# How an MoE stage numbers its slots and gathers its small experts: sixteen dealt pieces, rows at partitions 32 to 95

## The reference

```python
scores = sigmoid(x @ w_router)                     # 520 x 64
# of 8 groups of 8 experts the best 4 are kept, then the best 8 experts of a token
idx    = top_k(where(group_kept, scores + bias, -inf), 8)
gates  = w_sel / sum(w_sel) * 2.5
for each expert e, for each token t that chose it:
    y[t] += gate * (silu(x[t] @ w1[e]) * (x[t] @ w3[e])) @ w2[e]     # 1024 -> 256 -> 1024
```

## Time and profile before

| | us |
|---|---|
| median of three runs | 1242.86 |
| the profiled execution | 1241.34 |
| its span, from first to last instruction | 1239.5 |
| PE busy in the span | 1145.6 (92%) |
| PEld / DVE / ACT / POOL busy | 763.2 / 411.7 / 257.2 / 175.6 |

### The profile page before, as it was taken

One profiled execution on the slowest core, in us unless ns is written; L12 is line 12 of the kernel. 1 busy time (PEld: TensorE's weight loads), 2 busy tenths in 40 slices (PEclk: granted clock), 3 DMA queues, 4 the chain that ended last, 5 costly groups with the idle time before them and its releaser, 6 DMA issues.

```text
span 1239.5 us, 21052 instructions
## 1 busy us (share of the span) xinstructions
PE 1145.6 (92%) x8302; PEld 763.2 (62%) x8302; DVE 411.7 (33%) x1016; ACT 257.2 (21%) x564; POOL 175.6 (14%) x208
## 2 busy tenths in 40 slices
PE   7999997999987999889999899998999989989965
PEld 6888645877865688567656565555555556555411
DVE  0359997122067325711221111111211212111124
ACT  1101324022051315011222222221212212212200
POOL 3120040000000000202122122122221222211100
PEclk9999998999999999899999999999999999999977
DMA  9530304034048352619999999999999999999496
GB/s 330 226 136 1 153 12 170 1 135 153 1 141 322 132 216 91 241 51 337 358 378 375 369 376 379 368 376 358 370 370 359 373 378 358 376 359 363 182 357 268
DMA packets 66313, 319.16 MB, mean 257 GB/s; under 512 B 10473, under 2 KB 16833, under 8 KB 39629
## 3 DMA queue, kind: packets, MB, share of 16 engines
q1 hardware_dynamic: 51269, 278.60, 59.5%
q0 software_dynamic: 13568, 35.48, 8.4%
q10 hardware_dynamic: 1424, 4.35, 0.9%
HBM read 300.15 MB, written 29.36 MB: 266 GB/s over the span
## 4 chain that ended last, share of the span: by engine, by line
PE 68%; DMA 15%; DVE 14%; SPq 1%; issue 1%; ACT 1%; DVEq 0%; POOLq 0%
PE psum L744 62%; DMA arena<-in_w_e_dram 10%; DVE act_mem L1698 7%; PE psum L759 6%; DMA arena<-y_rows 3%; DVE mk_mem L1857 2%; DMA arena<-in_w_in_dram 1%; SPq L539 0%; DVE act_mem L1795 0%; DVE act_mem L1712 0%; DVE rstd L1786 0%; DVE act_mem L1793 0%; DVE act_mem L1763 0%; SPq L494 0%; SPq L493 0%
## 5 line engine op out<-in xcount | busy, mean ns | idle before, releaser
L744 PE MATMUL psum<-arena,act_mem 128*32 128x128 f32 (+6 forms) x4800 | 517.0, 365 | 20.8 <-DMA arena<-in_w_e_dram 16.5
L744 PEld LDWEIGHTS psum<-arena,act_mem 128*32 128x32 f32 (+5 forms) x4800 | 266.3, 125 | 210.7 <-issue 118.6
L744 PE MATMUL psum<-act_mem,arena 128*128 128x260 f32 (+1 forms) x1728 | 352.7, 366 | 9.2 <-DMA arena<-in_w_o_dram 3.8
L744 PEld LDWEIGHTS psum<-act_mem,arena 128*128 128x128 f32 x1728 | 306.2, 192 | 53.0 <-DMA arena<-in_w_o_dram 4.7
L759 PE MATMUL psum<-ident,act_mem 96*128 96x96 f32 (+8 forms) x484 | 77.7, 291 | 19.1 <-POOL ident L557 6.8
L667 POOL DMA_INDIRECT y_rows<-act_mem,idx_y x40 | 45.2, 1130 | 323.1 <-DVE idx_x L2074 173.0
L2086 DVE TENSOR_SCALAR act_mem<-psum,act_mem 96x512 f32<-96x512 f32 (+1 forms) x40 | 29.9, 748 | 156.0 <-PE psum L744 156.0
L1698 DVE SCALAR_TENSOR_TENSOR act_mem<-act_mem,wcb 128x511 f32<-128x511 f32 (+29 forms) x120 | 77.7, 725 | 0.0
L759 PEld LDWEIGHTS psum<-ident,act_mem 96*128 96x128 f32 (+8 forms) x484 | 57.5, 175 | 32.3 <-issue 8.0
L2083 DVE TENSOR_TENSOR act_mem<-act_mem,psum 128x192 f32<-128x192 f32 x35 | 12.4, 354 | 191.9 <-ACT act_mem L1554 191.9
L744 PEld LDWEIGHTS psum<-act_mem 128*96 128x96 bf16 (+4 forms) x371 | 28.6, 126 | 57.4 <-issue 51.4
(11 more groups left out here) (262 smaller groups left out, 698.0 us busy)
## 6 DMA issues: line engine op xcount, KB each, us to landing
arena<-in_w_e_dram SPq DMA_DIRECT2D x192, 1024.0 KB
arena<-y_rows SPq DMA_DIRECT2D x8, 2048.0 KB, 23.7
arena<-in_w_in_dram SPq DMA_DIRECT2D x16, 512.0 KB, 18.7
arena<-in_cache_mem_k_dram SPq DMA_DIRECT2D x8, 1024.0 KB, 8.5
arena<-in_cache_mem_v_dram SPq DMA_DIRECT2D x8, 1024.0 KB, 11.4
arena<-in_w_v_dram SPq DMA_DIRECT2D x1, 4096.0 KB, 24.3
arena<-in_w_k_dram SPq DMA_DIRECT2D x1, 4096.0 KB, 13.8
arena<-in_w_out_dram SPq DMA_DIRECT2D x1, 4096.0 KB, 13.8
```

Of the source, the lines that this page charges most:

```text
L744: return pe.matmul(out, lhsT, rhs, start=first, stop=last)
```

## The change

There are three edits.

1. **Dealt slots.** The row of slot numbers is no longer 0, 1, 2, ... With `LANES = 16` and a capacity cap, partition e * (cap/16) + j (e from 0 to 15, j from 0 to cap/16 - 1) gets slot e + 16 j. Sixteen equal pieces of consecutive partitions are dealt the slots like cards. An expert with 65 tokens in 96 slots filled partitions 0 to 64 before; now each of the sixteen pieces of 6 partitions holds 4 or 5 tokens. The layout depends on cap, so the 96-slot experts get a row of numbers of their own, `slots_m`, written over `mean_c`; before they used the first 96 of `slots`. `slots2` is dealt in each half.
2. **Rows at partitions 32 to 95.** The gather of a light expert writes its 64 rows to partitions 32 to 95 of `xg` rather than 0 to 63.
3. **Taken out on PE.** `turn_few` can no longer transpose a corner of 64 partitions. It multiplies all 128 partitions of `xg` by columns 32 to 95 of the identity, as a plain matmul. The partitions outside 32 to 95 hold old rows, which meet zeros. A semaphore increment on PE that nothing waited for (`m_few`) goes.

```diff
+LANES = 16
+FEW_AT = 32
-SORT_CONSTS = 11 + 2 * NB
+SORT_CONSTS = 13 + 2 * NB
...
+        slots_m = mean_c[:, 0:MCAP]
...
-            gp.iota(slots, pattern=[[1, CAP]], base=0, channel_multiplier=0, allow_small_or_imprecise_dtypes=True).then_inc(s_late, 1)
+            gp.iota(slots.rearrange("p (e j) -> p e j", e=LANES), pattern=[[1, LANES], [LANES, CAP // LANES]], base=0,
+                    channel_multiplier=0, allow_small_or_imprecise_dtypes=True).then_inc(s_late, 1)
...
-            number(slots2.rearrange("p (h s) -> p h s", h=2), [[0, 2], [1, LCAP]], 0)
+            for h in range(2):
+                number(slots2[:, LCAP * h:LCAP * h + LCAP].rearrange("p (e j) -> p e j", e=LANES),
+                       [[1, LANES], [LANES, LCAP // LANES]], 0)
+            number(slots_m.rearrange("p (e j) -> p e j", e=LANES), [[1, LANES], [LANES, MCAP // LANES]], 0)
...
-            def gather(n, b, s, cap=CAP):
+            def gather(n, b, s, cap=CAP, at=0):
                 gp.indirect_dma_start(
-                    out=xg[b][0:cap, :], out_offset=None, in_=x2_rows[:, :],
+                    out=xg[b][at:at + cap, :], out_offset=None, in_=x2_rows[:, :],
...
-                gather(n, n % 4, m_g[n % 4], LCAP if is_light(n) else CAP if is_big(e) else MCAP)
+                if is_light(n):
+                    gather(n, n % 4, m_g[n % 4], LCAP, FEW_AT)
+                else:
+                    gather(n, n % 4, m_g[n % 4], CAP if is_big(e) else MCAP)
...
             def turn_few(n):
                 for k in range(KC):
-                    last = turn(psum[:, 1, LCAP * k:LCAP * k + LCAP], xg[n % 4][0:LCAP, k:D:KC], LCAP)
+                    last = mm(psum[:, 1, LCAP * k:LCAP * k + LCAP], xg[n % 4][:, k:D:KC],
+                              ident[:, FEW_AT:FEW_AT + LCAP], True, True)
                 return last
...
-                if is_light(n):
-                    pe.sem_inc(m_few, 1)
...
-                    oh(n, e, slots[:, 0:cap], cap).then_inc(m_oh, 1)
+                    oh(n, e, slots if is_big(e) else slots_m, cap).then_inc(m_oh, 1)
```

More of the change, by code:

```diff
@@ L364, in decoder_step @@
         m_ht = sem("m_ht")
-        m_few = sem("m_few")
         m_hc = sem("m_hc")
@@ L625, in _ @@
                 number(both[:, :, :, k], [[0, 2], [len(LIGHT), E // NB]], len(HEAVY) * (E // NB) + j)
-            number(slots2.rearrange("p (h s) -> p h s", h=2), [[0, 2], [1, LCAP]], 0)
+            for h in range(2):
+                number(slots2[:, LCAP * h:LCAP * h + LCAP].rearrange("p (e j) -> p e j", e=LANES),
+                       [[1, LANES], [LANES, LCAP // LANES]], 0)
+            number(slots_m.rearrange("p (e j) -> p e j", e=LANES), [[1, LANES], [LANES, MCAP // LANES]], 0)
             gp.memset(far2, 2 * FAR).then_inc(s_sortc, 1)
-            gp.wait_ge(s_sortc, 6 + NB)
+            gp.wait_ge(s_sortc, 8 + NB)
             for k in LIGHT:
@@ L635, in _ @@
             gp.memset(rank_at[0:E, E:2 * E], -1.0).then_inc(s_sortc, 1)
-            gp.wait_ge(s_sortc, 9 + 2 * NB)
+            gp.wait_ge(s_sortc, 11 + 2 * NB)
             gp.memset(rank_at[E:2 * E, 0:E], -1.0).then_inc(s_sortc, 1)
```

## The result

| | before | after |
|---|---|---|
| time, median of 4 runs each | 1242.28 us | 1337.94 us (1329.83 to 1339.08) |
| ratio | | 1.0752, 95% interval 1.0728 to 1.0775 |
| profiled span | 1239.5 us | 1335.3 us |
| mean granted clock of TensorE | 0.975 | 0.948 |

The account below looks back on a forecast made before the run. DMA engines set the pace before, PE after. 1241.34 - 19.8 - 8.3 - 1.0 + 22.6 = 1234.8 us for a profiled run, 1236.4 us with 1.5 for the median; range 1231.6 to 1242.1.

Parts of the forecast that it names:

- 16 x 0.119 + 0.07 = 1.97 us: New light turn on PE: 16 loads at 0.119 us each, 0.94 us more per turn, 22.6 us over 24 light experts.
- bounds of 0.106 to 0.134 per load: Price of a load in the new light turn: 17.8 us more in all at the lower bound, 28.3 at the upper.
- Rival B: Light turn costs far more than its loads elsewhere; at 0.160 per load 38.4 us more, 1252.2 us; chance 0.12.
- break-even of 1.21 us per turn: Added cost per light turn at which the 29.1 us won from waits is used up, 0.136 per load.
- The clock at 1.00 throughout the experts: Sign in the new profile: with the waits for weights gone, PE's granted clock stays up through all experts.
- PE's own need: PE's time per eight experts without waits: 74.9 us before, 77.7 after, above the DMA engines' 70 to 76.6.
- -19.8 - 8.3 - 1.0: Savings on PE: waits for weights 19.8 us, slow `up`s at low clock behind them 8.3, waits for gathered rows 1.0.
- The rule of the Trainium skill that spoke against the edit: A logical transpose should use transpose, which skips the arithmetic; by it alone the edit loses 22.6 us.
- Rival A: DMA engines stay at 80 us per eight experts, as dealing evens nothing out or DRAM limits: 1246.0 us; chance 0.18.
- rival C: Cheaper on both sides: loads at 0.106, part of the turn hidden behind `up`: 1231.6 us or 1229; chance 0.10.
- an indirect DMA cuts its partitions into 16 consecutive pieces: Inference on gathers: the last 5 pieces are empty for an average expert; dealing takes 3.3 us per eight experts away.
- the light rows at 32 to 95 slow the weights less: Possibility: rows on both sides of partition 64 remove some of the 7.3 us of slow DMA stretches per eight experts.

Follow-up runs that it names:

- e8: The changed kernel with each plain matmul of a light turn streaming all 128 identity columns instead of 64: 1312.87 us.
- e5: The changed kernel with only four of the eight plain matmuls in each light turn: 1234.66 us.
- e7: The changed kernel with the light turns' loads at strides of 1, 2 and 4 elements instead of 8: 1288.22 us.
- e9: The changed kernel with the light turns' loads at strides of 3, 4 and 1 elements instead of 8: 1296.64 us.
- e3: The changed kernel with each light turn made by eight transposes of all 128 partitions, ACT copying columns 32 to 95 of each: 1210.69 us.
- e1: The kernel before with dealt slots alone; light rows stay at partitions 0 to 63 and are turned by transposes: 1222.58 us.
- e11: The dealt kernel with eight full transposes per light turn, light rows at partitions 64 to 127 instead of 32 to 95: 1222.01 us.
- e2: The kernel before with the plain matmul in the light turn alone; slots not dealt, rows at partitions 0 to 63: 1361.72 us.

## Why the prediction was wrong

**The step that failed** is the term "16 x 0.119 + 0.07 = 1.97 us" and its bounds of 0.106 to 0.134 per load. The turn took 4.04 us on average, 0.25 per load. The mechanism in it was right (16 loads, and loads set the pace: e8, e5); the price of one was read from rows of plain loads at another stride, and the stride's surcharge from transposes. The 64 loads in 7.61 us of the earlier trace rows are the `up` of a 112-slot expert, which reads its weights as `wu[:, j // 2, k, j % 2:FE:2]`, at a stride of 2; the 10 in 1.19 us are at a stride of 1. Both cost 0.119, and e7 shows the same for these two, 0.125 and 0.13; the price rises from 3 on (e9). The upper bound was the worse fault: no row of a plain load at a stride of 8 stood in the trace, so nothing there bounded it from above. Rival B had the right side and named the stride; its other reason, the passes of other matmuls that run up against the turn, is in no run. But its price of 0.160 was chosen just above my own bound, and its chance of 0.12 was too low for a break-even of 1.21 us per turn.

**Two consequences were not in the sum at all.** The balance, from e3 (1210.69) to the changed kernel (1337.94), which differ in the turn and ACT's copy of it alone, 127.3 us (they ran beside different runs of before, 1244.05 and 1242.28):

| term | worked out | us |
|---|---|---|
| slow turn | 24 x (4.08 - 1.16) | 70.1 |
| low clock behind it | e8 against the changed kernel | 25.1 |
| stalls | waits after | 19.7 |
| low clock behind the stalls | 5 x (8.15 - 5.82) | 11.7 |
| sum | | 126.6 |

"The clock at 1.00 throughout the experts" was false in a way that the prediction could have asked about: PE is never idle in the turn, and its clock falls all the same behind 18 of the 24. Why it falls there and not behind the other six stays open. And I counted the added instructions only as work. That 48 more in a loop could make PE load its program again did not occur to me, though the page gives the instruction queue (q8) a row of its own.

**What was right.** The waits for weights go with the dealing and the placing, and PE is the bound afterwards. PE's own need is 74.9 per eight experts: e3 shows 75.0 to 75.2, with the clock up and no wait for weights. The terms -19.8 - 8.3 - 1.0 with 24 x 0.13 for the full transposes would have given 1241.34 - 29.1 + 3.1 = 1215.3 and with the 1.5 us of the median 1216.8; measured 1210.7. So the gain was undersized by some 6 us, and I cannot name them. The 1.0 us for gathered rows is no part of the gain: in e3 PEld still waits 2.9 us for them, in four waits, where it was 2.3. The rule of the Trainium skill that spoke against the edit (Perfetto Trace Analysis, "Transposes") points the right way too: transposes turn in 1.16 us what takes 4.08 as a matmul. Rival A (DMA engines stay at 80 us) is refuted by e1 and e3, which move 386 and 394 to 397 GB/s where the kernel before moved 370 to 374, rival C by every turn. That an indirect DMA cuts its partitions into 16 consecutive pieces stays an inference: e1 shows that dealing gains 21.5 us, not how the pieces lie. That the light rows at 32 to 95 slow the weights less was held possible in the prediction; e3 and e11, 1210.7 against 1222.0 us, show it.

**The better kernel.** e3 keeps the first two parts and turns with transposes: 1210.69 us, 2.6% below the kernel before (interval 2.3 to 2.9%).

## What to carry to other kernels

Before an operation takes the place of another, look for a row with its exact access pattern, stride included; if there is none, the bound is open above, and the surcharge of a related instruction is not a bound. Count what an edit adds to a loop's instructions as well as to its work, and look at the instruction queue's packets. A gather that shared the DMA engines with a stream of weights was cheapest here where its rows fell evenly on both halves of the partitions.

## What the runs showed of the hardware

- A plain float32 matmul that loads 128 columns: 0.125 us per load at a stride of 1 element (2.00 us for 16), 0.13 at 2, 0.19 at 3, 0.25 at 4 and at 8. A float32 transpose of 128 columns stays at 0.14 to 0.15 us (1.09 to 1.23 for 8) at strides 1, 2, 4 and 8.
- TensorE can be busy without a gap and still have the lower clock behind it: the turn from 864.41 us ran at 1.00 and the `down` behind it at 0.67, and 18 of the 24 `down`s behind such turns were slow. Behind all 24 turns of e8 (4.07 us, 128 columns streamed per load instead of 64) they ran at full pace.
- A PE loop of 1615 instructions ran without being loaded again, and its jump back took 0.2 us; at 1663 each jump back took some 6 us, and PE stood still for 3.8 to 4.1 us in each (up to 5.5 in the other kernels of that length, e2), five times.
- 64 gathered rows per light expert beside a stream of weights: 1210.7 us with the rows at partitions 32 to 95, 1222.6 at 0 to 63, 1222.0 at 64 to 127.
